# Hybrid decoder step on one core: two conditioning loads, the order at the end of the GLA core and in the sample attention, and products of constants in three pauses

## The chip, the cores and the metric

The kernel runs on one NeuronCore of a Trainium2 chip. The metric is the device time of one execution in microseconds; lower is better. An execution of the kernel before took 1698.36 us in the median of 3 runs (1695.97 to 1700.7).

## The reference

One inference step of a trunk of two layers, for a prompt of 256 tokens and 8 samples of one token each, width 1024. Each layer is a token mixer and then a mixture of experts; both are conditioned by a vector of each sequence.

```python
for i in range(DEPTH):                                   # 2 layers
    sh1, sc1, gt1, sh2, sc2, gt2 = split(silu(c) @ w_ada[i] + b_ada[i], 6)
    h = rms_norm(x, norm_mix[i]) * (1 + sc1) + sh1
    m = gla_mixer(h) if i == 0 else dsa_mixer(h)         # prompt and samples apart
    x = x + gt1 * m
    x = x + gt2 * moe_ffn(rms_norm(x, norm_ffn[i]) * (1 + sc2) + sh2)
y = rms_norm(x, norm_final)
# gla, a sample: S = exp(g) * S + k v^T ; o = q S ; out = rms_norm(o) * silu(r) @ w_out
# dsa, a sample: top 256 of 2049 keys by an indexer, softmax(q k + bias) v over them, @ w_out
```

`silu(c) @ w_ada` of a layer is 1024 x 6144, eight items of 768 columns. Items 0 to 2 hold shift and scale of the mixer's norm, items 3 and 4 with part of 2 and 5 the mixer's gate and the second shift.

## The kernel before

All five engines run programs of their own, written out by hand, that wait for each other on semaphores. Activations lie transposed (features on partitions, 264 tokens in the free dimension). Weights go through a ring of four slots; SP issues the loads in one order, and a load waits until the slot's last user has freed it. `plan` gives slots out in the order in which it is called, so the order of its calls in the list of `it_ada` (conditioning items) and `it_gla` (four projection items of 768 columns) is the order of the loads.

**Conditioning.** An item costs TensorE `pe_ada_rows` (24 products, 32 columns of weights each, 48 passes in the profile), two copies by ScalarE into `mrow` (`act_ada`), `pe_ada_fold` (six products against a constant that add the four partial sums) and one addition by VectorE into `modT` (`dve_ada`). A product of fp32 is two passes, so two rows in counts of the profile.

**Start.** TensorE does items 0 to 4 one after the other, as they land. VectorE needs items 0 to 2 for the modulated input `hT`, which it writes in eight chunks. Then `pe_gla` multiplies `hT` with the 16 gate columns (L737), VectorE copies, and TensorE multiplies by the second gate matrix (L741).

**Projections.** 24 tiles of 128 columns, eight products of 264 tokens each (L757). Items 5, 6 and 7 stand between tiles: rows behind tile 5, 11 and 13, folds behind 7, 13 and 15. ScalarE computes softplus and exponents meanwhile, VectorE evicts and scans.

**GLA core.** From tile 16 on, a step of the core stands behind each tile (`pe_gla_core`): turns, scores, state updates, `pe_across` (queries against the state of the chunk before). The samples have an outer product (`pe_outer`), an update of their state by VectorE (`dve_sample`) and a product with the query (`pe_sample_o`) each. ScalarE takes squares and roots of the norm of two halves of the prompt (T = 0, 1) and of the samples (T = 2), and the last gates (`gate(22)`, `gate(23)`, Silu). The normalised rows `on` are turned (`pe_turn_on`) and multiplied by the gate (`dve_mix`) into `oT`, and `pe_out_proj` (L910) follows. POOL loads and stores the samples' states.

**Layer 1.** The prompt attention goes over eight tiles (2 halves, 4 heads of keys): `logits`, `turn_probs`, `mix_values`, with VectorE and ScalarE between. POOL gathers the picked keys and values of the samples in the meantime. Item 6 of layer 1 has its rows at `it == 8` of that loop and its fold behind it. Then the picked keys are turned (`turn_rows`), the samples' logits computed, softmax by VectorE and ScalarE (first pause of TensorE), value products, the choice of each head's own values by VectorE (second pause), and the output projection.

`pe_warm(n)` multiplies constants by constants, n products of 256 columns into bank 7, which nobody reads.

## Time and profile before

| | |
|---|---|
| time, median of 3 runs | 1698.36 us |
| lowest, highest | 1695.97, 1700.7 us |
| time of the profiled execution | 1698.2 us |
| its span, first to last instruction | 1696.4 us |
| granted TensorE clock, mean of the span | 0.977 |
| TensorE (matmul) busy | 1613.6 us |
| VectorE, ScalarE, POOL busy | 707.2, 447.6, 146.9 us |
| MB over DMA | 552.38 |

Times in rows are microseconds from the first instruction. A line number is that of the kernel before. "PE" is TensorE's matmul, "DVE" VectorE, "ACT" ScalarE. `x48` is a number of instructions (passes). In brackets stands the idle time of the engine ahead of the group and what ended it. The granted clock is 1.00 at 2.4 GHz and 0.50 at 1.2 GHz.

### The profile page before, as it was taken

To read this page: it belongs to the slowest core of one execution; us is meant where nothing else is said; L and a number is where in the kernel's file an instruction comes from. 1 tells how busy PE (TensorE), PEld (TensorE's weight loads), DVE (VectorE), ACT (ScalarE), POOL (GpSimd) and SP (SyncE) were. 2 spreads that over 40 slices of the span, in tenths; PEclk is the share of its full clock that TensorE was granted. 3 is DMA by queue.
4 is the path that set the end of the run, shared out by engine and by line. 5 is a ranking of instruction groups with operands and counts; after the bars stand their busy time and mean duration, and the time that the engine had idled before them with its cause. 6 is when DMAs were issued, how large, how long until landed. Compare 5 with 4: busy or idle time off the path is not lost. (4 is left out here: it accounts for less than half of the span.)

```text
span 1696.4 us, 30818 instructions
## 1 busy us (share of the span) xinstructions
PE 1613.6 (95%) x11730; PEld 953.5 (56%) x11730; DVE 707.2 (42%) x1918; ACT 447.6 (26%) x997; POOL 146.9 (9%) x208
## 2 busy tenths in 40 slices
PE   6999899999999999999989988989999999999997
PEld 4678576555555455555466755755555555545554
DVE  2133536463333333334246952276433333333334
ACT  2211221222222232222232133122222222223223
POOL 0001300000000000000020052000000000000000
PEclk9899899999999999999999988899999999999999
DMA  9975648799999999999584344459999999999990
GB/s 358 362 262 170 257 149 323 311 385 404 417 416 416 417 409 416 412 417 415 196 311 145 130 160 128 156 188 372 398 410 417 416 417 414 413 417 415 413 366 26
DMA packets 139032, 552.38 MB, mean 326 GB/s; under 512 B 19407, under 2 KB 36637, under 8 KB 104662
## 3 DMA queue, kind: packets, MB, share of 16 engines
q1 hardware_dynamic: 120562, 513.82, 76.3%
q0 software_dynamic: 15392, 34.66, 5.7%
q10 hardware_dynamic: 3012, 3.00, 0.5%
q8 instruction: 45, 0.74, 0.2%
q14 instruction: 21, 0.17, 0.0%
HBM read 562.74 MB, written 8.60 MB: 337 GB/s over the span
## 5 line engine op out<-in xcount | busy, mean ns | idle before, releaser
L1445 PE MATMUL PS<-ring,arena 128*64 128x256 f32 x4288 | 490.7, 382 | 2.6 <-ACT arena L1775 1.5
L1445 PEld LDWEIGHTS PS<-ring,arena 128*64 128x64 f32 x4288 | 304.7, 137 | 182.2 <-issue 41.2
L1469 PE MATMUL PS<-ring,arena 128*64 128x512 f32 x1072 | 259.6, 605 | 1.4 <-ACT arena L1760 1.4
L1408 PE MATMUL PS<-arena 128*128 128x512 bf16 (+1 forms) x796 | 197.4, 384 | 0.0
L1677 DVE TENSOR_TENSOR arena<-arena,PS 128x128 f32<-128x128 f32 x134 | 38.6, 288 | 371.1 <-ACT arena L1758 365.1
L1661 DVE TENSOR_SCALAR arena<-arena 128x512 bf16<-128x512 f32 x130 | 62.8, 483 | 256.5 <-ACT arena L1769 256.5
L1768 ACT COPY arena<-PS 64x512 f32<-64x512 f32 x134 | 77.5, 578 | 302.2 <-PE PS L1469 302.2
L1469 PEld LDWEIGHTS PS<-ring,arena 128*64 128x64 f32 x1072 | 65.1, 136 | 120.4 <-issue 104.0
L1758 ACT ACTIVATE arena<-PS 128x128 f32<-128x128 f32 x134 | 37.2, 278 | 326.5 <-PE PS L1445 326.5
L1408 PEld LDWEIGHTS PS<-arena 128*128 128x128 bf16 (+1 forms) x796 | 69.6, 99 | 91.9 <-issue 27.7
L1399 PEld LDWEIGHTS PS<-cst,arena 128*128 128x128 f32 x552 | 72.1, 195 | 80.2 <-issue 78.3
L1788 POOL COPY arena<-arena 128x1 int32 (+1 forms) x71 | 14.5, 204 | 1139.1 <-PE PS L1399 934.4
L1399 PE MATMUL PS<-cst,arena 128*128 128x128 f32 x552 | 98.0, 300 | 2.0 <-ACT arena L1775 1.4
L1663 DVE SCALAR_TENSOR_TENSOR arena<-arena 128x512 f32<-128x512 f32 x130 | 97.7, 751 | 4.6
L1667 DVE TENSOR_TENSOR arena<-arena 128x512 bf16<-128x512 f32 x130 | 90.0, 692 | 4.5
L757 PE MATMUL PS<-hT,ring 128*128 128x264 f32 x384 | 90.3, 394 | 0.3 <-DVE modT L519 0.3
L1775 ACT COPY arena<-PS 128x512 f32<-128x512 f32 x135 | 79.5, 589 | 28.9 <-PE PS L1399 27.3
L757 PEld LDWEIGHTS PS<-hT,ring 128*128 128x128 f32 x384 | 73.2, 193 | 15.4 <-issue 2.8
L1769 ACT COPY arena<-PS 64x512 f32<-64x512 f32 x134 | 77.9, 582 | 1.6
L1790 POOL DMA_INDIRECT arena<-h_rows,arena x71 | 72.7, 1024 | 61.6 <-POOL arena L1788 58.3
L1760 ACT COPY arena<-PS 128x128 f32<-128x128 f32 x134 | 35.7, 266 | 138.3 <-PE PS L1457 138.3
L910 PE MATMUL PS<-shT,ring 128*128 128x264 f32 x256 | 64.0, 409 | 0.9 <-DVE shT L2420 0.6
(512 smaller groups left out, 1552.0 us busy)
## 6 DMA issues: line engine op xcount, KB each, us to landing
ring<-in_moe_w_gate SPq DMA_DIRECT2D x134, 1024.0 KB, 7.7
ring<-in_moe_w_up SPq DMA_DIRECT2D x134, 1024.0 KB, 10.0
ring<-in_moe_w_down SPq DMA_DIRECT2D x134, 1024.0 KB, 15.6
ring<-in_w_ada SPq DMA_DIRECT2D x32, 1152.0 KB
ring<-in_w_ada SPq DMA_DIRECT2D x16, 768.0 KB
ring<-in_gla_w_in SPq DMA_DIRECT2D x8, 1152.0 KB
ring<-in_dsa_w_in SPq DMA_DIRECT2D x6, 1024.0 KB
arena<-in_state_gla POOLq DMA_DIRECT2D x8, 512.0 KB, 8.6
```

What stands on the lines that cost most here:

```text
L757: m = pe.matmul(PS[:, b, 0:TOK], w8_[:, k, (m_ % 6) * P:(m_ % 6 + 1) * P], hT[:, k, 0:TOK], start=(k == 0), stop=(k == KT - 1))
L910: m = pe.matmul(PS[:, 4 + k % 4, 0:TOK], w3[:, kk, (k % 2) * P:(k % 2 + 1) * P], src[:, kk, :], start=(kk == 0), stop=(kk == KT - 1))
L1399: ins_ = pe.transpose(PS[:, 6, k * P:(k + 1) * P], xv[:, 4 * half + k, :], K["ident"])
L1408: ins_ = pe.matmul(PS[:, c, :], oh[:, T * P:(T + 1) * P], y[:, 512 * j:512 * j + 512], start=False, stop=True, skip_group_check=True)
L1445: m = pe.matmul(PS[64 * half:64 * half + 64, 5, 0:256].rearrange("p (g n) -> p g n", g=2), rows[:, k, CAP * b:CAP * b + CAP], gu[:, :, k, ...
L1469: m = pe.matmul(PS[64 * j:64 * j + 64, 7, :], hTt[b][:, kk * CAP:(kk + 1) * CAP], ring[:, s, 2, kk * D + 512 * j:kk * D + 512 * j + 512], ...
L1663: dve.scalar_tensor_tensor(out=ysb[par][:, q], in0=ysb[par][:, q], scalar=wv[:, par:par + 1], in1=yw[:, 0, q], op0=ALU.mult, op1=ALU.subtr ...
L1667: dve.tensor_tensor(yw[:, 2, q], ysb[par][:, q], yw[:, 1, q], ALU.subtract).then_inc(M(l, "split"), 1)
L1768: act.copy(ysb[par][q, 0:512], PS[0:CAP, 7, :])
L1769: act.copy(ysb[par][q, 512:D], PS[CAP:P, 7, :]).then_inc(M(l, "ysb"), 1)
L1775: act.copy(xgT[into][:, 4 * half:4 * half + 4, :].rearrange("p k c -> p (k c)"), bank(6)).then_inc(M(l, "xgT"), 1)
L1790: pool.indirect_dma_start(out=xg[into], out_offset=None, in_=hrow_d[l], in_offset=IndirectOffsetOnAxis(ap=gi[:, into:into + 1], axis=0), b ...
```

## The change

Items 3 and 4 of layer 0 are loaded behind the first projection item, and their rows and folds stand between projection tiles, each fold one or two tiles behind its rows. In the GLA core, across(3), `pe_outer(1)` and `pe_outer(2)` move ahead of tile 23; `gate(23)` moves behind the squares of T = 1; sample products, turns and gate products have a new order; POOL issues the load of state 4 ahead of `scale_gate(1)`. In layer 1 the rows of item 6 move behind the attention loop, to banks 0 and 4, the fold behind two turns of keys, and the turned keys use banks in another order. `pe_warm(3)` is added at three places: ahead of the turn of the samples' normalised rows, of the turn of the sample probabilities, and of the turn of the chosen values.

```diff
@@ -310,12 +310,11 @@
...
-        it_ada = [plan(5), None]
+        it_ada = [plan(3), None]
         it_gla = []
-        for _ in range(3):
+        for n_ada in (2, 2, 1, 0):
             it_gla += plan(1)
-            it_ada[0] += plan(1)
-        it_gla += plan(1)
+            it_ada[0] += plan(n_ada)
         it_gout = plan(2)
@@ -725,8 +724,7 @@
...
                 load_wide(item, w_in, 768 * i)
-                if i < 3:
-                    sp_ada(0, [5 + i])
+                sp_ada(0, ((3, 4), (5, 6), (7,), ())[i])
             for i, item in enumerate(it_gout):
@@ -740,7 +738,7 @@
...
             m.then_inc(S("gla_pe"), 1)
-            pe.wait_ge(S("mod_T"), 5)
+            pe.wait_ge(S("mod_T"), 3)
             for m_ in range(24):
@@ -761,16 +759,17 @@
...
                     pe.sem_inc(S(f"slot_used{item[0]}"), 1)
-                    if m_ == 5:
-                        pe.wait_ge(S("softplus"), 1)
-                        pe_ada_rows(0, 5, 4)
-                    if m_ == 11:
-                        pe_ada_rows(0, 6, 4)
-                if m_ == 13:
-                    pe_ada_fold(0, 6, 4)
-                    pe_ada_rows(0, 7, 4)
+                if m_ == 3:
+                    pe.wait_ge(S("softplus"), 1)
+                    pe_ada_rows(0, 3, 4)
+                if m_ in (5, 11, 13):
+                    i = (m_ + 1) // 2 if m_ > 5 else 4
+                    pe_ada_fold(0, i - 1, 4)
+                    pe_ada_rows(0, i, 4)
                 if m_ == 7:
-                    pe_ada_fold(0, 5, 4)
+                    pe_ada_fold(0, 4, 4)
+                if m_ == 9:
+                    pe_ada_rows(0, 5, 4)
                 if m_ == 15:
@@ -818,10 +817,10 @@
...
                 pe_outer(0)
-            elif step == 7:
                 pe.wait_ge(S("state"), 4)
+                pe_across(3)
                 pe_outer(1)
-                pe_across(3)
+                pe_outer(2)
@@ -852,22 +851,24 @@
...
         def pe_gla_rest():
-            pe_outer(2)
+            pe_outer(3)
             pe.wait_ge(S("proj_act"), 8)
...
             pe_sample_o(0)
+            pe_turn_on(1, 0, 2, 2)
             pe_sample_o(1)
-            pe_outer(3)
+            pe_outer(4)
+            pe_turn_on(1, 1, 3, 2)
             pe_turn_on(0, 1, 1, 1)
-            pe_turn_on(1, 0, 2, 2)
-            pe_turn_on(1, 1, 3, 2)
             pe_sample_o(2)
-            for b in range(4, DEC):
+            pe_sample_o(3)
+            for b in range(5, DEC):
                 pe_outer(b)
...
             pe_sample_o(DEC - 1)
+            pe_warm(3)
             pe.wait_ge(S("on_ready"), 3)
@@ -942,10 +943,8 @@
...
                 ins_.then_inc(S("proj_dve"), 1)
-                if m_ == 9:
-                    dve_ada(0, [5], 4)
-                if m_ == 15:
-                    dve_ada(0, [6], 4)
+                if m_ in (6, 8, 12, 15):
+                    dve_ada(0, [{6: 3, 8: 4, 12: 5, 15: 6}[m_]], 4)
                 if m_ == 5:
@@ -998,12 +997,13 @@
...
             dve_on(1)
-            dve_mix(0, 0, 1)
             dve_sample(3)
-            dve_mix(0, 1, 1)
-            dve_mix(1, 0, 2)
-            dve_mix(1, 1, 3)
-            for b in range(4, DEC):
+            dve_mix(0, 0, 1, 1)
+            dve_mix(1, 0, 2, 2)
+            dve_sample(4)
+            dve_mix(1, 1, 3, 3)
+            dve_mix(0, 1, 1, 4)
+            for b in range(5, DEC):
                 dve_sample(b)
@@ -1038,10 +1038,10 @@
...
-        def dve_mix(T, half, b):
+        def dve_mix(T, half, b, turned):
...
             dve.wait_ge(S("r_scaled"), half + 1)
-            dve.wait_ge(S("on_turned"), 2 * T + half + 1)
+            dve.wait_ge(S("on_turned"), turned)
             dve.tensor_tensor(oT[:, 4 * half:4 * half + 4, T * P:(T + 1) * P], bank(b).rearrange("p (j t) -> p j t", t=P),
@@ -1065,14 +1065,15 @@
...
             act.activation(eg, Lg[:, :, SEQ:TOK], ACT.Exp, scale=-1 / 16)
+            act_ada(0, [3], 4)
             act.wait_ge(S("gla_dve"), GD["dL"] + 1)
...
             act.activation(ke, dL, ACT.Exp, scale=1 / 16).then_inc(S("exps"), 1)
-            act_ada(0, [5], 4)
+            act_ada(0, [4], 4)
             act.wait_ge(S("gla_dve"), GD["dE"] + 1)
...
             act.activation(cL, cL, ACT.Exp, scale=-1 / 16).then_inc(S("exps"), 1)
-            act_ada(0, [6, 7], 4)
+            act_ada(0, [5, 6, 7], 4)
             def gate(m_):
@@ -1081,7 +1082,6 @@
...
                     gate(22)
-                    gate(23)
                     act.wait_ge(S("on_ready"), 1)
@@ -1093,6 +1093,8 @@
...
                     act.activation(oms[:, 0:1], oms[:, 0:1], ACT.Sqrt, bias=K["eps"], scale=1 / GDV).then_inc(S("o_rms"), 1)
+                if T == 1:
+                    gate(23)
                 if T > 0:
@@ -1115,10 +1117,10 @@
...
                 load_state(b)
-            scale_gate(1)
             pool.wait_ge(S("state"), 4)
...
             load_state(4)
+            scale_gate(1)
             pool.dma_start(outs["gla_p"][0, 0].rearrange("h d v -> d h v"), Sst[1]).then_inc(S("out_pool"), 16)
@@ -2143,16 +2145,14 @@
...
                     logits(it)
-                if it == 8:
-                    pe.wait_ge(S("logit_sb"), 8)
-                    pe_late_rows(6, 0)
                 if it == 2:
...
                     mix_values(it - 3)
-            pe_late_fold(6, 5, 0)
+            pe.wait_ge(S("logit_sb"), 8)
+            pe_late_rows(6, 0, 4)
             dve_at(pe, "oht")
@@ -2165,14 +2165,16 @@
...
                     for h in range(2):
-                        m = pe.transpose(PS[:, 4 + b % 4, (2 * Pq + h) * P:(2 * Pq + h + 1) * P], Kg[:, h, b, P * Pq:P * Pq + P], K["ident"])
+                        m = pe.transpose(PS[:, 4 + (b + 1) % 4, (2 * Pq + h) * P:(2 * Pq + h + 1) * P], Kg[:, h, b, P * Pq:P * Pq + P], K["ident"])
                 m.then_inc(S("krow_T"), 1)
             turn_rows(0)
-            pe.wait_ge(S("mod_T"), 15)
             turn_rows(1)
+            pe_late_fold(6, 4, 256)
             dve_at(pe, "Qs")
...
             for b in range(DEC):
+                if b == 1:
+                    pe.wait_ge(S("mod_T"), 15)
                 if b + 2 < DEC:
@@ -2187,6 +2189,7 @@
...
             pe.wait_ge(S("att_o_sb"), 2)
+            pe_warm(3)
             dve_at(pe, "sprob")
@@ -2206,6 +2209,7 @@
...
             pe.sem_inc(S(f"slot_used{hold_v[0]}"), 1)
+            pe_warm(3)
             dve_at(pe, "osel")
@@ -2394,7 +2398,7 @@
...
             ins_.then_inc(S("dsa_dve"), 1)
-            dve_late(6, 5, 0)
+            dve_late(6, 4, 256)
             pe_at(dve, "slogit")
@@ -2500,12 +2504,11 @@
...
                     exps(it)
-                elif it == 8:
-                    act_late_rows(6, 0)
                 probs_out(it - 2)
...
                         act.dma_start(dst, src).then_inc(S("kv_out"), 16)
+            act_late_rows(6, 0, 4)
             mixed_out(1)
@@ -2513,7 +2516,7 @@
...
                     act.wait_ge(S("klogit"), b - 3)
-                act.copy(KTs[b % 4][:, :, 0:256], bank(4 + b % 4).rearrange("p (q n) -> p q n", q=2))
+                act.copy(KTs[b % 4][:, :, 0:256], bank(4 + (b + 1) % 4).rearrange("p (q n) -> p q n", q=2))
                 act.copy(KTs[b % 4][:, :, 256], kT[:, :, SEQ + b]).then_inc(S("krow_sb"), 1)
@@ -2566,7 +2569,7 @@
...
             sp_setup()
-            sp_ada(0, range(5))
+            sp_ada(0, range(3))
             sp_gla()
@@ -2590,7 +2593,7 @@
...
             pe_ada_fold(0, 0)
-            pe_ada(0, range(1, 5))
+            pe_ada(0, range(1, 3))
             pe_gla()
@@ -2614,7 +2617,6 @@
...
             dve_modulate(0, 0)
-            dve_ada(0, [3, 4])
             dve_gla()
@@ -2632,7 +2634,7 @@
...
             act_norm(0, norm_sq, 3, between=lambda: act_ada(0, [0]))
-            act_ada(0, range(1, 5))
+            act_ada(0, range(1, 3))
             act_gla()
...
             act_shift(1, 0, 1)
```

## Rows read from the trace of the kernel before

**Rows 1.** Stretch 40 to 60 us: busy time and instructions of each engine, clock, DMA share, GB/s.
```profile
40.00:60.00 20.00, 15.61 (x153) 9.16 (x146) 4.11 (x15) 2.98 (x7) 0.00 (x0) 0.83 1.03 401
```

**Rows 2.** TensorE by lines, 64 to 138 us: busy us, mean ns, idle before.
```profile
L757 PE MATMUL PS<-hT,ring 128*128 128x264 f32 x260 | 61.1, 396 | 0.3 <-DVE modT L519 0.3
L440 PE MATMUL PS<-ring,cT 128*32 128x256 f32 x144 | 8.4, 381 | 0.6 <-PE PS L757 0.6
L451 PE MATMUL PS<-cst,mrow 128*128 128x9 f32 x36 | 4.3, 252 | 0.7 <-DVE modT L519 0.7
```

**Rows 3.** TensorE in order of time at the start: start us, us, idle before.
```profile
43.99 5.35 PE L440 MATMUL PS<-ring,cT 128*32 128x256 f32 x48 [1.06 <-DMA ring<-in_w_ada]
...
57.22 3.73 PE L737 MATMUL PS<-hT,arena 128*16 128x264 f32 x16
61.54 2.04 PE L741 MATMUL PS<-arena 16*128 16x264 f32 x8 [0.58 <-DVE arena L936]
63.51 23.31 PE L757 MATMUL PS<-hT,ring 128*128 128x264 f32 x96
```

**Rows 4.** VectorE in order of time, the modulation of the first norm.
```profile
44.12 2.67 DVE L649 TENSOR_SCALAR hT<-hT,modA,modT 128x256 f32<-128x256 f32 x8
```

**Rows 5.** Stretches of 4 and 2 us, as rows 1; the clock is third from the right.
```profile
44.00:48.00 4.00, 4.00 (x40) 1.94 (x44) 2.79 (x9) 0.00 (x0) 0.00 (x0) 0.50 1.03 402
...
64.00:68.00 4.00, 4.00 (x13) 3.15 (x12) 0.00 (x0) 3.96 (x7) 0.00 (x0) 0.63 1.03 400
...
200.00:202.00 2.00, 2.00 (x16) 0.54 (x12) 1.38 (x5) 0.00 (x0) 0.78 (x2) 0.53 1.04 411
...
1058.00:1060.00 2.00, 2.00 (x24) 0.75 (x24) 0.00 (x0) 0.00 (x0) 0.00 (x0) 0.50 0.70 218
```

**Rows 6.** Lines, 178 to 216 us, the end of the GLA core.
```profile
L1053 DVE SCALAR_TENSOR_TENSOR arena<-arena,eg,PS 128x256 f32<-128x256 f32 x32 | 13.2, 476 | 6.0 <-PE PS L882 5.9
L882 PE MATMUL PS<-arena 8*128 8x256 f32 x64 | 10.5, 450 | 0.1
...
L888 PE MATMUL PS<-arena,rstd 128*8 128x256 f32 x64 | 6.0, 468 | 0.9 <-DVE arena L1053 0.8
...
L897 PE MATMUL PS<-cst,ring 128*128 128x128 f32 x16 | 2.2, 278 | 1.7 <-DVE shT L1045 1.7
```

**Rows 7.** TensorE in order of time, from the last turn to the router.
```profile
208.64 0.69 PE L873 MATMUL PS<-cst,hT 128*128 128x128 f32 x2 [1.70 <-DVE hT L1010]
209.71 12.94 PE L910 MATMUL PS<-shT,ring 128*128 128x264 f32 x48 [0.38 <-DVE shT L1013]
...
244.68 3.19 PE L614 MATMUL PS<-cst 128*128 128x256 f32 x14
```

**Rows 8.** ScalarE in order of time, the roots of the GLA norm.
```profile
189.91 1.28 ACT L1091 ACT_TABLE_LOAD   x1
191.21 0.30 ACT L1091 ACTIVATE modA<-modA,cst 128x4 f32<-128x4 f32 x1
...
207.58 0.29 ACT L1095 ACTIVATE modA<-modA,cst 128x1 f32<-128x1 f32 x1
```

**Rows 9.** TensorE in order of time, attention and sample attention of layer 1.
```profile
1022.04 2.49 PE L538 MATMUL PS<-ring,cT 128*32 128x256 f32 x36
1025.35 2.58 PE L538 MATMUL PS<-ring,cT 128*32 128x256 f32 x12 [0.82 <-issue]
1031.58 1.94 PE L2116 MATMUL PS<-cst,arena 128*128 128x128 f32 x8 [3.66 <-remote]
...
1042.39 1.13 PE L2180 MATMUL PS<-arena 128*128 128x257 f32 x4
...
1055.50 0.41 PE L2192 MATMUL PS<-cst,arena 128*128 128x128 f32 x2 [2.25 <-DVE arena L2404]
...
1058.22 3.61 PE L2205 MATMUL PS<-ring,arena 128*16 128x256 f32 x32
1063.73 0.69 PE L2211 MATMUL PS<-cst,arena 128*128 128x128 f32 x2 [1.90 <-DVE arena L2416]
1064.97 13.67 PE L910 MATMUL PS<-shT,ring 128*128 128x264 f32 x48 [0.55 <-DVE shT L2420]
```

## The prediction

> **What bounds it.** I read the stretches of 20 us first. At 40 to 60 the DMA engines are full and TensorE has pauses [rows 1]. From 64 to 138, in the projections, the lines view gives TensorE idle times of 0.3, 0.6 and 0.7 us in all [rows 2]. So the start is set by loads and short chains, the projections by TensorE alone. Then I read the order of time where the diff touches it: TensorE's at the start [rows 3], with VectorE's chain there [rows 4] and the granted clock [rows 5]; the end of the GLA core by lines and in order [rows 6, 7], with ScalarE's part [rows 8]; and the sample attention of layer 1 [rows 9]. The reader should see that every edit is of a few microseconds, against 1696.4 us of span.
>
> **1. Two conditioning items leave the start.** TensorE has folded item 2 at 42.93 (43.99 less the wait of 1.06) and starts the first projection at 63.51 [rows 3], 20.6 us later. Between them lie rows and folds 3 and 4, up to 57.22, partly at half clock, the gate input (3.73), its copy (0.58) and the second gate product (2.04) [rows 3].
> The rows go away from there, but they hid VectorE's chain: it has the first modulated chunk at 44.12 + 0.33 = 44.45 and the last at 46.79 [rows 4]. So TensorE stands from 42.93 to 44.5. From there on it has the gate input and product, which use 16 of the array's 128 columns or rows. The clock is at 1.2 GHz in 44 to 48 although dense rows run there (0.50), and it is there again in 64 to 68 (0.63), just behind the same two gate products [rows 5]. So I take them at 1.2 GHz, twice as long: 44.5 + 7.4 + 0.6 + 4.1 = 56.6. At 2.4 GHz it is 44.5 + 3.7 + 0.6 + 2.0 = 50.8. The loads do not hold them: item 3 landed at 43.99, where its rows started with a wait on DMA [rows 3], and its place in the queue then has the first projection weight.
> The projections thus start 6.9 us (at most 12.7) earlier. The same rows and folds are then paid for inside them, with their copies hidden by products: 8.4 / 3 = 2.80 and 4.3 / 3 = 1.43 each [rows 2], 8.4 for both items. The first projections lose about 1.4 now: 23.31 for 96 passes [rows 3], where 96 at full clock take 22. Behind a longer stretch of little work I give them 2.0. Sum: -6.9 + 8.4 + 0.6 = **+2.1**. Bounds: -12.7 + 8.4 - 1.4 = -5.7, and +4.5 if half clock lasts for the first three projections (11 us at full clock's work, some 4.4 lost).
> Loads in the projections: by the DMA rate of 401 GB/s [rows 1] an item of 3.1 MB takes 8 us. The tightest is item 7: its slot comes free behind projection 11 at about 114, it lands at about 124, and rows 7 want it at about 127. SP's queue is in the order in which slots come free, so nothing behind it is blocked. VectorE takes the folds right behind its evictions, and ScalarE copies rows 3 where it would wait for VectorE anyway. Nothing for either; without that cover each fold waits about 1.1, as the start has it.
>
> **2. The end of the GLA core.** Now projection 23 stands between `pe_outer(0)` and across(3), and TensorE waits 1.7 for VectorE's product with the gate [rows 6]. After, across(3) and two outer products go ahead of projection 23. TensorE then waits 0.8 for state 3, which the projection covered; in exchange ScalarE's squares for the second half start 4.2 us earlier, that half is ready at 190.4 instead of 193.4, and the wait of 1.7 goes. I laid the instructions out: outer 1.06 and sample product 0.55 at full clock, twice that at half (their means here are 10.5 / 8 = 1.3 and 6.0 / 8 = 0.75), VectorE 13.2 / 8 = 1.65 for a sample [rows 6]. The last sample product then ends at 203.9 at full clock, or 205.3 if the clock falls at 200 as it did [rows 5]. Now it ends at 206.94 (208.64 less the wait of 1.70 [rows 7]). That is -1.6.
> Against it: gate 23 (Silu) now stands between ScalarE's last two square roots. Now the root behind the last sample product starts at 207.58 with no table load ahead. After, it needs its table again, 1.28 as at 189.91 [rows 8], and nothing hides it: **+1.3** on the chain that ends in `mix_in`. The load that gate 23 needs runs while projection 23 does.
> The Trainium skill, page "ScalarE: Activation LUTs", sections "What ACT_TABLE_LOAD costs" and "Table sets: the hidden batching unit", says to do all of one table set before changing, since a change costs about 1.28 us of load and 1.38 of drain; this speaks against moving gate 23. The row has a root 0.02 us behind the end of the load and shows no drain [rows 8]; by the page this part would be 1.4 us longer.
> Three products of constants are six passes: seven products take 3.19 [rows 7], so three take 1.37 at full clock and 2.7 at half. They stand in the pause before the turn (1.70 now, 3.0 after), hidden either way. The output projection starts at half clock now: 12.94 for 48 passes [rows 7], where full clock's 0.233 makes 11.2, 1.8 lost. I give the products one chance in four to return it: -0.4. Part 2 together: -1.6 + 1.3 - 0.4 = **-0.7**, bounds -3.5 and +1.5.
> POOL issues the load of state 4 ahead of its gate scaling; it lands at about 193.5, before sample 4 wants it at 195. The stores start some 4 us later and end before ScalarE needs them for the next norm; if they did not, the norm's products still have one projection (3.7) of slack.
>
> **3. Rows of item 6 behind the attention loop.** If TensorE ran through, the present order would have rows from 1022.04 to 1024.84, then turns, copies and value products in turn, and the first sample logits at 1033.8. After the change TensorE stands from 1022.1 to 1023.65 for VectorE's probabilities, ends the loop at 1029.6, then has rows (2.80), turns of one-hots (0.6), two turns of keys (1.0), fold (1.4) and one turn more: 1035.85. So the move itself costs **+2.05**: the rows filled a pause and now fill none. The banks (4 and 0 instead of 0 and 1, the keys' banks turned by one) let turns begin before the copies are out; that is in the 1035.85.
> But the trace shows the logits at 1042.39, not 1033.8. In the rows TensorE stops: 12 of its 48 passes start only at 1025.35, and the next work is at 1031.58, with releasers "issue" and "remote" [rows 9]. That is 6.4 us of stop (1031.58 less 1024.84, less the 0.35 that copies would ask), and the half clock behind it adds 2.2 to what the same work takes at full clock. No engine or load of the trace accounts for it. I can't say if it belongs to this place (beside POOL's gathers of values, whose last issue ends at 1030.5) or to the chip's moment. If it stays, or strikes elsewhere, the difference is the 2.05. If it goes with the move, it is 2.05 - 8.4 = -6.3. I take the first: rows of the same form ran three times in the projections at 381 ns a pass with no such stop [rows 2], but nothing says why the move should end it.
>
> **4. Products in the two pauses of the sample attention.** The first pause is 2.25 (softmax), the second 1.90 (choice) [rows 9]. Against them stand 1.37 of products at full clock, hidden, or 2.7 at half, which delays the choice by 0.8. What they may return: the value products take 3.61 at half clock (0.50 in 1058 to 1060 [rows 5]) with 1.70 ahead of them, 2.6 lost, and the output projection's first 48 passes take 13.67 instead of 11.2, 2.5 lost [rows 9]. The products bring work into just the stretch after which the clock falls, but behind them come some 5 us with 8 or 16 columns. I take one chance in three that all 5.1 comes back, and else 0.7: **-2.2**, bounds -5.1 and +0.8.
> The Trainium skill, "TensorE: Matmul & The Clock Gate", section "What's actually happening", says that the throttled state is the default and that activity releases it. By it the products would hold the clock through the pauses; this is rival C.
>
> **Sum.** +2.1 - 0.7 + 2.05 - 2.2 = +1.2. The profiled execution took 1698.2, 0.16 below the median; 1698.36 + 1.2 = **1699.5**.
>
> **Rivals.**
> A. *The stop in the rows of item 6 goes with the move.* For it: these rows alone lie beside the gathers, and the profiled execution with its stop took no longer than the median, so the timed runs seem to have it too. Against: nothing shown ties it to the place. +1.2 - 8.4 = -7.2: 1691.2.
> B. *The gate products set the start, and half clock stays.* Place: TensorE from 42.9 to the third projection. For it: the only work there uses 16 columns. Against: in 64 to 68 the clock was back within one projection [rows 5]. Part 1 is +4.5, part 4 returns nothing: +4.5 - 0.7 + 2.05 = +5.9: 1704.3. It decides once the first three projections take more than 15 us.
> C. *The products of constants hold 2.4 GHz at all three places*, and the stop stays: part 2 -2.4, part 4 -5.1: 2.1 - 2.4 + 2.05 - 5.1 = -3.4: 1695.0.
>
> **Chances.** The forecast's own case 0.47, A 0.33, B 0.10, C 0.10. 0.3% of the time is 5.1 us, about what a measurement tells from no change. A passes it in 8 of 10 (0.27), C in 2 of 10, with part 1 low (0.02), the own case in 1 of 50 (0.01): faster 0.30. B passes in 7 of 10 (0.07), the own case in 1 of 25 (0.02): slower 0.09. Same: 0.61. The range takes in most of A (1691.2 less 3) and B: 1688.0 to 1704.5. The own case alone has 1696 to 1703.
>
> **What would show it.** First projection at about 56 with gate products at half clock, fold 7 done some 2 us later. No wait at the product with the gate, a table load between the last square and root, 4.0 instead of 2.8 us from the last sample product to the output projection. The rows of item 6 with or without a gap that nothing releases: this alone moves the time by 8. Value products at 0.5 or 1.0 of the clock. The forecast is wrong if the stop vanishes, or if the gate products keep 2.4 GHz.

## The result and the profile after

| | before | after |
|---|---|---|
| time, median of 8 runs each, us | 1698.84 (1694.61 to 1704.33) | 1690.86 (1688.15 to 1693.16) |
| time of the profiled execution, us | 1698.2 | 1690.48 |
| span, us | 1696.4 | 1688.6 |
| granted clock, mean | 0.977 | 0.978 |

The ratio of the two sets of runs is 0.9946, interval 0.9932 to 0.996: 9.2 us faster (the two medians of the table lie 8.0 apart). In a later set of runs the same kernel stood at 0.9931 (0.9915 to 0.9946). The forecast was 1699.5, 1.2 us slower than before; rival A's time was 1691.2.

TensorE at the start, in order of time, after (the same work as [rows 3]):

```profile
41.16 1.78 PE L450 MATMUL PS<-cst,mrow 128*128 128x9 f32 x12 [1.12 <-ACT mrow L513]
44.68 5.87 PE L735 MATMUL PS<-hT,arena 128*16 128x264 f32 x16 [1.74 <-DVE hT L648]
51.13 2.04 PE L739 MATMUL PS<-arena 16*128 16x264 f32 x8 [0.58 <-DVE arena L937]
53.11 14.51 PE L755 MATMUL PS<-hT,ring 128*128 128x264 f32 x64
```

Its clock there, busy time of each engine in stretches of 4 us, clock third from the right:

```profile
46.00:50.00 4.00, 4.00 (x13) 1.44 (x12) 0.80 (x3) 0.00 (x0) 0.00 (x0) 0.62 1.03 401
50.00:54.00 4.00, 3.42 (x15) 2.24 (x14) 0.42 (x1) 0.74 (x1) 0.00 (x0) 1.00 1.03 401
54.00:58.00 4.00, 4.00 (x20) 3.42 (x19) 0.43 (x1) 3.96 (x7) 0.00 (x0) 1.00 1.03 402
```

TensorE waits for `hT` until 44.68, as worked out (44.5). The gate input starts at half clock: the granted clock is 0.50 in each stretch from 44 to 49 and 0.97 from 49 to 50. So it takes 5.87, between the 3.7 of full clock and the 7.4 that I took, and the clock rises while it runs. The second gate product runs at 2.4 GHz (2.04, as before, and not 4.1). The first projection starts at 53.11, 10.4 earlier than [rows 3], and the clock does not fall behind the gate products: 64 passes take 14.51.

The end of the GLA core, TensorE and then ScalarE, after (against [rows 7, 8]):

```profile
201.68 1.04 PE L889 MATMUL PS<-arena,rstd 128*8 128x256 f32 x8 [0.78 <-DVE arena L1053]
202.65 2.93 PE L613 MATMUL PS<-cst 128*128 128x256 f32 x6
205.70 0.60 PE L874 MATMUL PS<-cst,hT 128*128 128x128 f32 x2
```

```profile
203.13 0.19 ACT L1094 ACTIVATION_READ_ACCUMULATOR hT<-PS 128x1 f32 x1
203.34 1.28 ACT L1095 ACT_TABLE_LOAD   x1
204.63 0.29 ACT L1095 ACTIVATE modA<-modA,cst 128x1 f32<-128x1 f32 x1
```

The table load stands between square and root, as forecast: 1.28, with 0.02 us ahead of it and 0.01 behind it, so no drain shows. The output projection starts at 206.68, 3.96 behind the last sample product's end (4.0 forecast).

Layer 1, TensorE, after (against [rows 9]):

```profile
1023.22 1.09 PE L2118 MATMUL PS<-cst,arena 128*128 128x128 f32 x8 [1.56 <-issue]
...
1028.40 2.40 PE L2129 MATMUL PS<-arena 128*64 128x128 f32 x32
1030.72 2.80 PE L537 MATMUL PS<-ring,cT 128*32 128x256 f32 x48
...
1036.77 1.03 PE L2182 MATMUL PS<-arena 128*128 128x257 f32 x4
...
1051.80 2.91 PE L2208 MATMUL PS<-ring,arena 128*16 128x256 f32 x32
1054.87 2.09 PE L613 MATMUL PS<-cst 128*128 128x256 f32 x6 [0.16 <-PE PS L2208]
...
1057.72 10.95 PE L911 MATMUL PS<-shT,ring 128*128 128x264 f32 x48 [0.55 <-DVE shT L2424]
```

The rows of item 6 run through in 2.80; the stop of about 6 us is gone. The 1.56 ahead of 1023.22 is another wait: part 3 had TensorE stand 1.55 there for VectorE's probabilities, and two of the later traces, with 1.52 at this place, name VectorE. The first logits start at 1036.77 and not at 1042.39. The output projection's first 48 passes take 10.95 (2.4 GHz) where they took 13.67.

### The profile page after: what moved, and what is told of

Same layout as the page of the kernel before. It is cut to its first block and busy times, and to the rows that moved or that the text cites. A ratio compares the mean times of both kernels' runs of the same rounds, so it can differ in the third digit from the quotient of the medians.

```text
span 1688.6 us, 30856 instructions
## 1 busy us (share of the span) xinstructions
PE 1616.7 (96%) x11748; PEld 956.6 (57%) x11748; DVE 707.1 (42%) x1918; ACT 449.9 (27%) x999; POOL 146.7 (9%) x208
## 5 line engine op out<-in xcount | busy, mean ns | idle before, releaser
L911 PE MATMUL PS<-shT,ring 128*128 128x264 f32 x256 | 59.3, 387 | 0.9 <-DVE shT L2424 0.5
## 6 DMA issues: line engine op xcount, KB each, us to landing
ring<-in_moe_w_gate SPq DMA_DIRECT2D x134, 1024.0 KB, 7.9
ring<-in_moe_w_up SPq DMA_DIRECT2D x134, 1024.0 KB, 10.2
ring<-in_moe_w_down SPq DMA_DIRECT2D x134, 1024.0 KB, 15.5
ring<-in_dsa_w_in SPq DMA_DIRECT2D x6, 1024.0 KB
```

## The experiments: the parts alone

The first four kernels are the one before with one part each, against it on the same chip (median 1701.1).

**Rows of item 6 alone** (the hunks of part 3; one is shown):

```diff
-                if it == 8:
-                    pe_late_rows(6, 0)
+            pe_late_rows(6, 0, 4)
```

> The kernel before with part 3 alone: the rows of item 6 of layer 1 behind the attention loop, the fold behind two turns of keys, the turned keys' banks by one further. Everything ahead of 1020 us is as before. My forecast (the stop of 6.4 us stays or strikes elsewhere): +2.05, so about 1701 where the kernel before has 1699. Rival A (the stop belongs to the place where the rows stood): -6.3, so about 1692.5; in the trace the first sample logits start at about 1037 instead of 1042.39, with no gap put down to issue or remote in or behind the rows. A third theory, that the stop is a matter of the moment: the trace of this kernel may or may not have it, and the ratio lies near +2.05 or between.

1696.42; ratio 0.9965 (0.995 to 0.998), so -5.9 (-8.5 to -3.4). Rival A's -6.3 is in it, my +2.05 is not. Its trace:

```profile
1028.80 1.15 PE L2127 MATMUL PS<-arena 128*64 128x128 f32 x16
1031.46 1.15 PE L2127 MATMUL PS<-arena 128*64 128x128 f32 x16 [1.51 <-issue]
1032.54 2.80 PE L538 MATMUL PS<-ring,cT 128*32 128x256 f32 x48
```

No stop of 6 us, but one of 1.51 ("issue") among the value products, which now stand beside the gathers, where the rows stood.

**Products of constants alone** (`+ pe_warm(3)` three times):

> The kernel before with the three groups of three products of constants alone. My forecast: -0.4 and -2.2, so -2.6. Rival C (they hold 2.4 GHz at all three places): -1.8 and -5.1, so -6.9. If they do nothing for the clock: 0 to +0.8. The rows of item 6 stand where they stood, so this trace also shows whether the stop of 6.4 us behind 1025 us comes again: if it belongs to the place it must be here too, with the first sample logits at about 1042.

1697.0; 0.9982 (0.9969 to 0.9995), -3.1 (-5.3 to -0.9): my -2.6 fits, rival C's -6.9 doesn't. In its trace both output projections take 10.95 for their first 48 passes, as rival C had it. The stop is there again:

```profile
1024.36 2.23 PE L538 MATMUL PS<-ring,cT 128*32 128x256 f32 x33
1027.56 1.81 PE L538 MATMUL PS<-ring,cT 128*32 128x256 f32 x15 [0.98 <-issue]
1033.12 1.06 PE L2117 MATMUL PS<-cst,arena 128*128 128x128 f32 x8 [3.75 <-remote]
```

**The start alone** (part 1: items 3 and 4 loaded behind the first projection item, rows and folds between tiles):

> The kernel before with part 1 alone: items 3 and 4 of layer 0 leave the start. My forecast: +2.1, with the first projection at 56.6 us and fold 7 some 2 us later than before. The low end of its bounds, the gate products at full clock, is the rival that the trace of the changed kernel speaks for: first projection at about 53, fold 7 about 3.4 us earlier, time -3.4. Rival B: +4.5. The rows of item 6 of layer 1 stand where they stood: if the stop belongs to the place, it is in this trace as well.

1698.44; 0.9984 (0.9971 to 0.9996), -2.7 (-4.9 to -0.7); +2.1 is outside. The stop is there (8 of the 48 passes start late, and TensorE stands for 4.44 us behind them, "remote").

**The GLA core alone** (order, gate 23, load of state 4; no products of constants):

> The kernel before with part 2 alone and without its products of constants: the order at the end of the GLA core, gate 23 between the last two square roots, the load of state 4 ahead of POOL's gate scaling. My forecast: -1.6 and +1.3, so -0.3: the last sample product ends 1.6 us earlier, and 4.0 us instead of 2.8 lie between it and the output projection. The trace of the changed kernel had that start 5.0 - 3.4 = 1.6 us earlier than before, less what the products of constants did. Rival: without the products of constants the clock falls here for as long as before, and the output projection's first 48 passes take 12.9 us or more. The rows of item 6 of layer 1 stand where they stood, as in the two runs ahead of this one.

1699.02; 0.9984 (0.9973 to 0.9995), -2.7 (-4.6 to -0.9), where I had -0.3. Its trace shows less: measured against the work ahead of this part, the last sample product ends 1.7 earlier and the output projection starts 0.4 earlier, with a wait of 2.98 between them ahead of the turn, and its first 48 passes take 13.11. The stop is there (TensorE stands for 4.11 behind the rows, "remote").

So all four traces with the rows at their old place (the kernel before among them) have the stop, which begins between 1024.0 and 1027.9 us, and neither trace with the move has it.

## The experiments: what the stop hangs on

In these four traces the stop begins just ahead of the fifth of POOL's last eight gathers of values, by 0.2 to 0.5 us, and TensorE's next work comes 0.2 to 1.2 us behind the end of the eighth gather's issue. In the kernel before it begins at 1024.53 and ends at 1031.58, and POOL has the fifth and the eighth gather at

```profile
1024.71 1.94 POOL L1956 DMA_INDIRECT ring<-in_cache_v,arena  x1 [0.30 <-issue]
...
1029.56 0.94 POOL L1956 DMA_INDIRECT ring<-in_cache_v,arena  x1 [0.30 <-issue]
```

A load of 16 KB of code (queue 8, "instruction", in the transfers view) also stands beside the start of the rows. Three kernels take these apart; theory 1 is that the gathers hold up this load of code and TensorE stops for want of it.

```diff
 e8:  pool_rows
+                    if h == 1 and name == "vg_in":
+                        pool.wait_ge(S("krow_T"), 1)
 e9, e10:  ahead of the attention, 64 or 128 times
+            pe.wait_ge(S("mod_T"), 3)
            dve_at(pe, "four_picked")
```

> The kernel before with one wait more: POOL issues the last eight gathers of values only once the first picked keys are turned, so none of them is under way while the rows of item 6 run (which stay where they were). Theory 1, formed from the traces of the first four kernels: at 1022.0 us a load of 16 KB of code starts for TensorE (queue 8 in the transfers view), the gathers that run beside it hold it up, and TensorE reaches the code that it brings about 97 records later, where it stops until 1031. Then the stop of about 6 us goes: the first sample logits at about 1036 instead of 1042.4, time about -6. Theory 2 (the stop belongs to the rows themselves at that place of the program, gathers or not): it stays, time 0. Theory 3: the late gathers hold up the next code load, and the stop comes back some 230 records later.

> The kernel before with 64 instructions more on TensorE ahead of the attention of layer 1: waits on a semaphore that has been raised long before, in a pause of 2.7 us, so about +0.5 by themselves. They move every later instruction by 64 places against the code blocks of 256 instructions. Theory 1: the code load now starts 64 records earlier in the work, at about 1016 to 1020 instead of 1022.0, and the stop in the rows of item 6 is several us shorter, with its place 64 records earlier (ahead of or at the start of the rows). Theory 2 (place in the work): the stop is as before, 36 or so passes into the rows, 6 us.

> The same with 128 instructions, half a code block; by themselves about +4. Theory 1: the code load that had started at 1022.0 starts 128 records earlier in the work, at about 1010 to 1014, and no stop stands in the rows of item 6; one of up to 2 us may stand some 130 records behind them. Theory 2: the stop is as before.

**Late gathers** (`krow_T` is raised when picked keys have been turned, so the gathers of values come 16 us later): 1695.18; 0.9976 (0.9956 to 0.9996), -4.1 (-7.5 to -0.7). The rows, at their old place, run through:

```profile
1026.27 2.80 PE L538 MATMUL PS<-ring,cT 128*32 128x256 f32 x48
1029.40 1.06 PE L2118 MATMUL PS<-cst,arena 128*128 128x128 f32 x8 [0.33 <-PE PS L538]
```

Everything here is 4.2 us late from earlier in the execution; less that, the first logits (1037.99) are at 1033.8, which is what I had laid out for a loop with no stop. Only the gathers were moved. They now lie beside the logit products, where TensorE has one wait of 0.73, put down to a copy by ScalarE; 0.65 and 0.67 in the two later kernels with late gathers.

**Code shifted**: single runs of 1701.58 and 1703.37. The code load moved as meant, from 1022 to 1019 to 1021 in the one with 64. Its transfers from 1019 to 1021:

```profile
q0 software_dynamic: 79, 0.20, 30.5%
q8 instruction: 1, 0.02, 2.7%
```

None comes between 1021 and 1040. The stop stayed beside the gathers:

```profile
1026.18 2.50 PE L538 MATMUL PS<-ring,cT 128*32 128x256 f32 x28
1029.53 3.64 PE L538 MATMUL PS<-ring,cT 128*32 128x256 f32 x20 [0.84 <-issue]
1035.98 1.94 PE L2116 MATMUL PS<-cst,arena 128*128 128x128 f32 x8 [2.81 <-remote]
```

With 128 the load came some 10 us ahead of the rows, and the rows, which met the gathers later in their group, still took 4.20 with a wait of 1.56 behind them. So theory 1 fell: the stop needs no load of code beside it. The Trainium skill, page "Runtime: NRT & Kernel Launch", section "Instruction fetch mechanics", has code come in blocks of 16 KiB ahead of use, mostly hidden. The trace's packets agree (45 on this queue, 0.74 MB in all), and so do both runs, in which the load moved and the stop stayed beside the gathers.

**The changed kernel with the rows back in the loop:**

> The changed kernel with part 3 alone undone: the rows and fold of item 6 back at their place, with the banks of before. Rival A, which the result speaks for: about 6 us over the changed kernel, so about -2 to -3 against the kernel before. My forecast's own case (the move costs 2.05): 2 us under the changed kernel. Theory 1 (code load held up by the gathers): TensorE's code is shorter ahead of this place by other parts' edits (24 records more than before up to here), so the stop stands some 24 records earlier in the work, and lasts 6 to 7 us.

1694.17; 0.9968 (0.9951 to 0.9985), -5.4: by the ratios 3.8 and 6.3 us less gain than the changed kernel had in its two sets, about what rival A says. But the profiled execution has no stop, which I had not expected. In it, half clock at 999 and 1019 had delayed TensorE, and the rows stood at 1028.43, where the last gather's issue (1028.21 to 1029.16) was already on; they took 3.26. Its twelve times lie widely (1686.8 to 1699.6). That says nothing about the stop: the three longest have a granted clock of 0.973, the others 0.977 to 0.981, and the kernel with late gathers, whose trace has no stop either, spreads almost as far (1691.4 to 1703.0) in the same way.

**The changed kernel with the gathers brought to the rows.** One wait on POOL, `S("probs"), 8`, at the same place as in the kernel with late gathers:

> The changed kernel with one wait more: POOL issues the last eight gathers of values only once all eight softmax tiles are normalised, so they run from about 1026 to 1037 and the rows of item 6, now at 1030.7, stand in their second half, as they did before the change. Theory 4 (the stop comes where dense rows of 128 x 32 meet the second half of these gathers, wherever the rows stand in the program): the stop comes back, the rows take 5 to 9 us instead of 2.8, and most of the gain of the changed kernel is lost: about +5 against it. Theory 2 (the stop belonged to the rows at their old place): rows of 2.8 us as in the changed kernel, time as there. VectorE's last operations of the attention (the one-hots, the fill of 2304 columns) are over before the second half of these gathers, so a stop would also acquit them.

TensorE is held up again, at the new place of the rows:

```profile
1031.67 1.98 PE L537 MATMUL PS<-ring,cT 128*32 128x256 f32 x32
1034.42 0.64 PE L537 MATMUL PS<-ring,cT 128*32 128x256 f32 x4 [0.78 <-issue]
1035.84 0.64 PE L537 MATMUL PS<-ring,cT 128*32 128x256 f32 x5 [0.78 <-issue]
1037.28 1.09 PE L537 MATMUL PS<-ring,cT 128*32 128x256 f32 x5 [0.80 <-issue]
1038.70 0.62 PE L537 MATMUL PS<-ring,cT 128*32 128x256 f32 x2 [0.33 <-issue]
```

The rows last from 1031.67 to 1039.32, 7.65 and not 2.80: behind the 32nd pass they come up to five at a time, 1.43 us apart. POOL has the fifth and the eighth gather at

```profile
1032.62 0.95 POOL L1960 DMA_INDIRECT ring<-in_cache_v,arena  x1 [0.30 <-issue]
...
1036.37 0.95 POOL L1960 DMA_INDIRECT ring<-in_cache_v,arena  x1 [0.30 <-issue]
```

The other engines in two stretches of it (TensorE, weight loads, VectorE, ScalarE, POOL):

```profile
1032.00:1034.00 2.00, 1.65 (x32) 0.72 (x24) 0.00 (x0) 0.00 (x0) 1.39 (x3) 1.00 0.26 94
1034.00:1036.00 2.00, 0.80 (x7) 0.32 (x9) 0.00 (x0) 0.00 (x0) 1.70 (x2) 1.00 0.46 129
```

VectorE and ScalarE do nothing, the DMA engines are busy to a quarter and a half, the clock is 1.00; only POOL issues gathers. So VectorE's operations at the end of the attention, which lay beside the stop before, are not needed for it. Whether they add to it isn't shown: here the passes trickle, while in the kernel before TensorE also stood still for 3.66 behind its last pass. Time: 1694.11, 0.9943 (0.9928 to 0.9959), 3.9 above the changed kernel without products and 5.5 above the one with an early table load, in the same set; against the changed kernel itself, in other sets (0.9946 and 0.9931), it can't be told apart, so against it the 5 us that I expected are not confirmed by time.

**What sets the start of the stop is open.** "The second half of the gathers" is one reading. The traces allow another: wherever gathers are under way, 28 to 40 passes of the rows go through before the first pause. That holds for the kernel before (36), products alone (33), start alone (40), core alone (36), the shifted codes (28 and 38), gathers on the rows (32), and for two traces in which the rows began beside the eighth gather: the changed kernel without products (31; its rows took 4.02) and the one with the rows back in the loop (28; 3.26). No kernel has rows beside the first four gathers alone, so the two aren't told apart. The first eight gathers of values (1007.97 to 1017.69 in the kernel before) lie beside logits and value products of the prompt, and TensorE has no pause over 0.4 us there.

## The experiments: the table load and the products of constants

```diff
 e6
                 if T == 1:
                     gate(23)
+                    act.activation(oms[:, 8:9], K["eps"], ACT.Sqrt)
 e11, e16 (the same kernel twice)
-            pe_warm(3)        (three times)
 e14: rows back in the loop, gathers late, the square root of e6
 e17: e14 without pe_warm(3)
```

> The changed kernel with a square root of a constant by ScalarE right behind gate 23, which nobody reads: the table load for the last root then stands while ScalarE has nothing else to do. My step (the load of 1.28 us ahead of the last root is on the chain): the pause between the last sample product and the output projection is 1.3 us shorter, 2.7 instead of 4.0, and the time 1.3 less than the changed kernel's. Rival: the products of constants, two of their six passes at half clock, then stand in the way, or another table load comes ahead of the root anyway: 0.

> A candidate for the best version: the changed kernel with the rows of item 6 back in the attention loop, where they fill a pause (my 2.05), the last eight gathers of values only once the first picked keys are turned, so that they do not meet the rows, and the early table load of the run ahead. If the stop comes only where rows and gathers meet: -2 to -3.5 against the changed kernel, so about 1688. Rival: the late gathers meet the logit products instead and cost there what the rows gain, as the 0.7 us wait at 1047 in the trace with late gathers hints: about 0.

> The changed kernel without its three groups of products of constants. Rival C's mechanism, for which the trace of the changed kernel speaks: +1.4 to +2.2 at the output projection of the first layer (its first 48 passes take 12.4 to 13.1 us instead of 10.95) and about +4 in the sample attention (value products 3.5 instead of 2.9, projection 12.6 to 13.7 instead of 10.95), so about +5 to +6 in time. My forecast priced them at 2.6.

These ran beside the kernel with the gathers brought to the rows (kernel before 1703.46). **Early table load**: 1688.58, 0.9914 (0.9901 to 0.9928). The load is off the chain, but TensorE gains only 0.3 at this place (3.66 behind the last sample product and not 3.96):

```profile
205.57 0.29 ACT L1095 ACTIVATE modA<-modA,cst 128x1 f32<-128x1 f32 x1
```

```profile
204.87 2.93 PE L613 MATMUL PS<-cst 128*128 128x256 f32 x6
207.59 0.64 PE L874 MATMUL PS<-cst,hT 128*128 128x128 f32 x2
```

The root is ready at 205.86, and the six passes at half clock keep TensorE until the turn at 207.59. The rival given with this run was right: what the load frees, the products take. Without the products the early load brings all of its 1.28: the output projection starts 4.05 behind the last sample product in the changed kernel without products, and 2.77 in the combined version without them. **Combined** (rows in the loop, late gathers, early load): 1687.39, 0.9903 (0.9888 to 0.9918), the best ratio, with first logits at 1033.77. **Without products**: 1690.18, 0.9927 (0.9913 to 0.994), no worse than the changed kernel had been; +5 to +6 was expected. That left open where their gain goes, so the pair ran side by side:

> The changed kernel again, to stand beside itself without the products of constants on the same chip. By its first result 9 us under the kernel before. In its trace I look for half clock behind the places where the products keep it away.

> The changed kernel without its three groups of products, again. Rival C: about 5 us over the changed kernel, with 12.4 us or more for the first 48 passes of both output projections. My price: 2.6 over it. Third theory, from the first run of this kernel: 0, because what the products gain at their places is lost again by half clock that comes later in the routers and at the end of the experts.

> The combined version (rows in the loop, late gathers, early table load) without the three groups of products. With them it stood 16.1 us under the kernel before. Rival C: about 5 us less gain, 11. Third theory: the same gain within about 1 us.

Against a kernel before of 1701.13: with the products 1689.36 and 0.9931 (0.9915 to 0.9946), without 1691.27 and 0.9938 (0.9925 to 0.9951), so they are worth 1.2 by the ratios, 1.9 by the medians, neither outside the measurement. The combined version without them has 1686.47, 0.9921 (0.9906 to 0.9937), which isn't told apart from the 0.9903 with them in another set. The traces of the pair show where TensorE gains and loses. Stretches of the changed kernel with products, then without:

```profile
258.00:268.00 10.00, 8.62 (x54) 6.60 (x47) 8.52 (x29) 0.96 (x2) 0.00 (x0) 0.68 1.03 419
828.00:838.00 10.00, 7.29 (x44) 4.67 (x41) 4.06 (x8) 1.70 (x4) 1.67 (x2) 0.83 0.90 352
...
1040.00:1080.00 40.00, 37.96 (x221) 30.30 (x220) 7.28 (x28) 5.77 (x16) 0.00 (x0) 1.00 0.64 216
```

```profile
258.00:268.00 10.00, 8.63 (x101) 5.97 (x94) 9.06 (x56) 1.91 (x4) 0.00 (x0) 1.00 0.89 316
828.00:838.00 10.00, 7.63 (x54) 4.66 (x53) 4.08 (x9) 2.73 (x7) 1.67 (x2) 1.00 0.92 347
...
1040.00:1080.00 40.00, 34.92 (x190) 26.30 (x189) 6.57 (x25) 5.92 (x17) 0.00 (x0) 0.87 0.54 170
```

At the first output projection the products bring 3.2 us (start of one later instruction in both traces, less the same at 190). In the router behind it the clock falls to 0.68 with them and stays at 1.00 without, and 2.4 are lost again. At the end of the layer's experts another 2.8 are lost, for two reasons. With products, then without:

```profile
831.15 5.36 PE L1447 MATMUL PS<-ring,arena 128*64 128x256 f32 x32 [2.02 <-DMA ring<-in_moe_w_down]
```

```profile
833.11 3.67 PE L1447 MATMUL PS<-ring,arena 128*64 128x256 f32 x32 [0.98 <-DVE arena L1691]
```

1.7 are half clock (5.36 against 3.67), and 1.0 is a longer wait, for a load of weights. What they gain in the sample attention (4.3, 1.00 against 0.87) is kept. So 7.5 are won and 5.2 given back. The first traces of either kernel have this pattern too.

That the products cause the later losses is not shown by more than these pairs. Over all seventeen traces, the longer wait (1.9 to 2.1, for `in_moe_w_down`) is in all seven with the products and in none of the ten without. The half clock behind that wait is in four of the seven and in none of the ten. The half clock in or just behind the router is in five of the seven, missing with the products alone and with the gathers on the rows, and it is also in four of the ten: the start alone (5.51 for 16 passes and not 3.83), both shifted codes, and the combined version without products.

## Why the prediction was wrong

**Part 3, the step "I take the first" (the stop stays or strikes elsewhere): this failed**, and it decides the sign. The term stood at +2.05; alone it measured -5.9. The rows I read had the key to it: the gathers' last issue ended at 1030.5, and the work behind the stop came at 1031.58 [rows 9]. I put the place and the chip's moment side by side and chose without a price for either. What the runs put in its place: the stop belongs to the meeting of these dense rows with the gathers, before and after the change alike. Of seven kernels with the rows at the old place and the gathers as they were, six traces had it (the two with shifted code among them) and the seventh reached the rows only at the last gather; moving the gathers away removed it, and bringing them to the new place held the rows up there. (By its own two terms, 6.4 and 2.2, the stop was worth 8.6, where the sum has 8.4.)

**The +2.05 itself** held in kind. With the rows in the loop and no stop the first logits are at 1033.8, as laid out. In the combined version they come 3.0 earlier than in the changed kernel (1033.77 against 1036.77), from a loop that is 0.45 late there: the move costs 3.45. The 1.4 beyond my term are in that trace half clock at 1025 to 1028 (16 value products 1.69 and not 1.15, the turns behind them 1.97 and not 1.09); the trace of the rows alone has no half clock there, but the wait of 1.51.

**Part 1: "I take them at 1.2 GHz" failed too.** I had the gate products at half clock throughout. The clock was at half when the gate input began, as before the change behind rows and folds, but it rose at 49 while the gate input ran; the second product kept its 2.04, which it had before as well [rows 3], and the projections behind them lost nothing (14.51 for 64 passes, 14.49 for as many at 98.34 before), where I gave them 2.0. With 53.11 for the start, -10.4 + 8.4 - 1.4 = -3.4, and fold 7 ends 3.4 earlier, where I had about 2 later; alone the part measured -2.7 and not +2.1.

**Part 2.** The chain is as written down: no wait at the product with the gate, the load of 1.28 ahead of the last root, 3.96 and not 4.0. The Trainium skill's 1.38 of drain ("ScalarE: Activation LUTs", "What ACT_TABLE_LOAD costs") doesn't appear here: 0.02 and 0.01 on the two sides of the load. The trace of this part alone has 0.4 earlier for the forecast 0.3; its timed -2.7 is more than that, and where the rest lies is open.

**Part 4 and the products.** -2.6 in all was the right size: -3.1 alone, 1.2 in the changed kernel, the latter not outside the measurement. But it was right for another reason. In the changed kernel both output projections ran at 2.4 GHz (10.95 for 48 passes). The Trainium skill, "TensorE: Matmul & The Clock Gate", section "What's actually happening", says that activity releases the throttle; the trace agrees in that the clock was 0.50 where the products ran (204 to 206, 1054 to 1056) and 0.98 and 1.00 in the 2 us behind. The second place is sure: 10.95 in all seven traces with the products, 12.60 to 13.67 in the ten without. The first is not: with the early table load the projection took 11.62, in the combined version 11.59, with the gathers brought to the rows 13.13. Rival C's gains of 6.9 were there at their places (7.5 in the pair), and its sum was still too high, because part of them was lost again later, for which I had no term.

**Sum.** The parts alone add up to -14.4, the whole measured -9.2 and -11.7. Each carries about 2 us of uncertainty, so I read no more into it. That rival A's 1691.2 lies within 1 us of the measured median is in part luck: its stop is right, but it kept +2.1 for part 1, which measured -2.7.

## What to carry to other kernels

A stop that the trace puts down to "issue" or "remote" is a price like any other: look at what every other engine issues beside it, POOL's indirect transfers above all, before calling it chance, since the largest term of a sum may hang on it. Keep dense matmuls of short instructions apart from a group of gathers, by moving either of the two; one wait on POOL (-4.1) did about as much here as a new place for 48 passes (-5.9). And compare a filler's gain at its place with a trace without it to the end of the layer, not to the end of the pause: here 7.5 at the places were 1.2 to 1.9 in time.

## What the runs showed of the hardware

- 48 passes of 128 x 32 take 2.80 us alone and 7.65 beside the gathers, the last sixteen in groups of up to five, 1.43 us apart, with VectorE and ScalarE idle and the DMA engines a quarter to a half busy. Value products (128 x 64) had a wait of 1.51 at the same spot in the trace of the rows alone. By which way the gathers reach TensorE stays open; no load of code and no work of VectorE or ScalarE is needed for it.
- The hold-up begins 28 to 40 passes into the rows; in the kernel before and in the three single parts that leave the rows in the loop, this is 0.2 to 0.5 us ahead of the fifth gather. Which of the two counts isn't shown.
- A table load of ScalarE costs 1.28 us and no more, where ScalarE waits anyway, and can be taken off the chain by an early use of the same function (4.05 to 2.77).
- The best version measured is the combined one, 1687.39 us with the products and 1686.47 without, 0.9903 and 0.9921 of the kernel before. It is not told apart from the changed kernel with the early table load (0.9914).
